# Modulations moved from a mixer's TensorE to three feed-forward stages' VectorE, memory keys moved into the inverse

## What is computed

```python
mod_lat = silu(c) @ w_mod + b_mod          # 1024 -> 6144, one row
mod_ctx = silu(c_ctx) @ w_mod + b_mod      # of this, only shift and scale before the mixer (2048) are used

def memory_cross_attention(h, m, w_q, w_kv, q_gain, k_gain, w_o):   # m = rms_norm(mem, xattn_mem_norm)
    q = rms_norm((h @ w_q).reshape(B, S, 4, 128), q_gain)
    kv = (m @ w_kv).reshape(B, M, 2, 4, 128)
    k, v = rms_norm(kv[:, :, 0], k_gain), kv[:, :, 1]
    s = einsum('bqhd,bkhd->bhqk', q, k) * 128 ** -0.5
    return einsum('bhqk,bkhd->bqhd', softmax(s), v).reshape(B, S, 512) @ w_o
```

## Time and profile before

| | |
|---|---|
| median of 3 runs | 2467.96 us (2465.76 to 2468.3) |
| span of the profiled execution | 2465.7 us, 41821 instructions |
| TensorE (PE) busy | 2246.6 us (91%) |
| weight loads (PEld), beside it | 2014.1 us (82%) |
| VectorE, ScalarE, GpSimd busy | 979.8, 1157.1, 1191.6 us |
| mean granted TensorE clock | 0.959 of full speed |
| DMA | 318.49 MB, 129 GB/s on the mean |

### The profile page before, as it was taken

The page is one execution under the profiler, slowest core; times in us unless marked ns, Lnnn a source line. Parts: engine busy times, 40 slices in busy tenths (PEclk is TensorE's granted clock), DMA queues, the critical chain, the costliest instruction groups (busy, mean ns, idle before and its releaser), DMA issues. The chain is left out here.

```text
span 2465.7 us, 41821 instructions
## 1 busy us (share of the span) xinstructions
PE 2246.6 (91%) x17916; PEld 2014.1 (82%) x17916; DVE 979.8 (40%) x1980; ACT 1157.1 (47%) x1651; POOL 1191.6 (48%) x304
## 2 busy tenths in 40 slices
PE   8998989899998999888989999897987777998998
PEld 7998865488998999785568999775866777998997
DVE  2321644324211220356242321256665777333540
ACT  5433632465433442543255543455883555553342
POOL 6774610074875877440053887332310000675784
PEclk9999999899999999999989999898998888999999
DMA  7554522253654555432333554331204111653552
GB/s 251 171 175 130 155 83 86 69 173 101 201 170 143 189 183 162 139 111 86 120 103 103 171 188 154 118 104 52 69 21 135 35 36 24 209 165 126 180 180 95
DMA packets 303958, 318.49 MB, mean 129 GB/s; under 512 B 7881, under 2 KB 295101, under 8 KB 303261
## 3 DMA queue, kind: packets, MB, share of 16 engines
q1 hardware_dynamic: 303773, 315.81, 39.8%
HBM read 312.58 MB, written 3.21 MB: 128 GB/s over the span
## 5 line engine op out<-in xcount | busy, mean ns | idle before, releaser
L370 POOL TENSOR_TENSOR slab_lo<-ring,slab_hi 128x2048 fp32r<-128x2048 f32 (+1 forms) x238 | 1073.5, 4527 | 762.7 <-ACT slab_hi L359 727.0
L359 ACT CAST slab_hi<-ring 128x2048 fp32r<-128x2048 f32 (+1 forms) x238 | 443.8, 1869 | 550.8 <-PE bank L440 278.8
L435 PE MATMUL bank<-ffn_h_hi,slab_hi 128*128 128x256 f32 x1344 | 331.2, 284 | 0.0
L436 PE MATMUL bank<-ffn_h_lo,slab_hi 128*128 128x256 f32 x1344 | 329.7, 283 | 0.0
L435 PEld LDWEIGHTS bank<-ffn_h_hi,slab_hi 128*128 128x128 f32 x1344 | 257.9, 192 | 0.5 <-issue 0.3
L436 PEld LDWEIGHTS bank<-ffn_h_lo,slab_hi 128*128 128x128 f32 x1344 | 258.0, 192 | 0.1
L402 PE MATMUL bank<-ffn_hidden_hi,slab_hi 128*128 128x256 f32 x704 | 199.3, 283 | 0.0
L403 PE MATMUL bank<-ffn_hidden_lo,slab_hi 128*128 128x256 f32 x704 | 199.2, 283 | 0.0
L404 PE MATMUL bank<-ffn_hidden_hi,slab_lo 128*128 128x256 f32 x704 | 199.2, 283 | 0.0
L440 PE MATMUL bank<-ffn_h_hi,slab_lo 128*128 128x256 f32 x1344 | 189.1, 283 | 4.4 <-POOL slab_lo L370 4.4
L440 PEld LDWEIGHTS bank<-ffn_h_hi,slab_lo 128*128 128x128 f32 x1344 | 173.3, 192 | 5.2 <-POOL slab_lo L370 5.2
(11 more groups left out here) (655 smaller groups left out, 5369.0 us busy)
## 6 DMA issues: line engine op xcount, KB each, us to landing
ring<-in_ffn_w_in SPq DMA_DIRECT2D x88, 1024.0 KB, 5.1
ring<-in_ffn_w_out SPq DMA_DIRECT2D x32, 1024.0 KB, 5.2
ring<-in_w_in SPq DMA_DIRECT2D x27, 1024.0 KB, 5.3
ring<-in_mix_w_in SPq DMA_DIRECT2D x24, 1024.0 KB, 5.4
ring<-in_w_mod SPq DMA_DIRECT2D x24, 1024.0 KB, 5.2
ring<-in_w_up SPq DMA_DIRECT2D x22, 1024.0 KB, 5.1
ring<-in_ffn_w_out SPq DMA_DIRECT2D x16, 768.0 KB, 4.4
ring<-in_mix_w_out SPq DMA_DIRECT2D x8, 1024.0 KB, 5.2
```

The lines of the kernel that those rows point to most:

```text
L359: act.copy(self.hi[i % self.PLACES][:, 0:w], K.ring[n % RING][:, 0:w]).then_inc(self.hi_ready, 1)
L370: pool.tensor_tensor(self.lo[i % self.PLACES][:, 0:w], place[:, 0:w], self.hi[i % self.PLACES][:, 0:w].bitcast(F32), ALU.subtract).then_in ...
L435: pe.matmul(out, w[0][:, k, col], act[0][:, k, :], start=(k == 0), stop=False)
L436: pe.matmul(out, w[0][:, k, col], act[1][:, k, :], start=False, stop=False)
```

## The change

1. The modulations leave the mixer. A new `Modulations` is given to three feed-forward stages (`mod_part` 0: ffn2 of layer 0, 1: ffn1 of layer 1, 2: ffn2 of layer 1). Each makes 2048 of the 6144 columns, in 16 pieces of 0.5 MB with two places of their own. VectorE adds weight tile times a scalar of `cs` into bank 7, and copies the sums out after a group is full; TensorE, after the stage's last output product, multiplies each 128 of these sums by a column of ones (`pe`), and VectorE copies the result. Part 0 makes both versions (latent and context) of the first 2048 columns, the other parts only the latent.
2. In the inverse's wait TensorE now projects the memory's keys: two slabs straight from the ring, as full float32 products (`feature_major`, L309), with the memory scaled by GpSimd (`MemoryKeys`). ScalarE copies them to `xkeys`.
3. The attention stage has no modulations in its steps, none ahead, no transposes behind, and loads no slabs.
4. The cross attention has 10 slabs: four of the output projection, values 0, queries 0 and 1, values 1 (half of it ahead of the steps, half in steps 0 and 1), two of the output. The sums of squares of keys come after the norm of x on ScalarE.

```diff
+class Modulations:
+    PIECES, PLACES = 16, 2
+    BANK = 7
+    def __init__(self, K, ctx, part):
+        self.K, self.part = K, part
+        self.both = part == 0
+        self.cols, self.groups = (HALF, 4) if self.both else (2 * HALF, 2)
+        self.a_group = KD // self.groups
+        self.count = self.PIECES // self.a_group
+        self.first = 0 if self.both else 2 * KD * part
+        self.place = [K.sb(f"mod_piece{i}", [P, self.groups, self.cols], ctx=ctx) for i in range(self.PLACES)]
+        self.sums = K.sb("mod_sums", [P, self.count, 2 * HALF], ctx=ctx)
...
+        again = part == 2
...
+    def eaten(self, p):
+        return self.base + p + 1 + p // self.a_group
+    def kept(self, g):
+        return self.base + (g + 1) * (self.a_group + 1)
+    def sync(self, sync, p):
+        K = self.K
+        g, h = divmod(p, self.a_group)
+        if p >= self.PLACES:
+            sync.wait_ge(self.steps, self.eaten(p - self.PLACES))
+        src = groups_of(K.a["w_mod_2"], h * self.groups, self.groups, self.first * P + g * self.cols, self.cols)
+        sync.dma_start(self.place[p % self.PLACES][:, :, :], src).then_inc(self.landed[p % self.PLACES], 16)
+    def dve(self, dve, p):
+        K, own, bank = self.K, self.K.dve_own, self.K.bank[self.BANK]
+        g, h = divmod(p, self.a_group)
+        dve.wait_ge(self.landed[p % self.PLACES], 16 * (self.landings + p // self.PLACES + 1))
+        for q in range(self.groups):
+            k, w = h * self.groups + q, self.place[p % self.PLACES][:, q, :]
+            for v in range(1 + self.both):
+                out = bank[:, v * self.cols:(v + 1) * self.cols]
+                if k == 0:
+                    last = dve.tensor_scalar(out, w, K.cs[:, k, v:v + 1], None, ALU.mult)
+                else:
+                    last = dve.scalar_tensor_tensor(out, w, K.cs[:, k, v:v + 1], out, ALU.mult, ALU.add)
+            if q < self.groups - 1:
+                own.after(dve, last)
+        last.then_inc(self.steps, 1)
+        dve.wait_ge(self.steps, self.eaten(p))
+        if h == self.a_group - 1:
+            dve.tensor_copy(self.sums[:, g, :], bank[:, :]).then_inc(self.steps, 1)
+            dve.wait_ge(self.steps, self.kept(g))
+    def pe(self, pe):
+        K, bank = self.K, self.K.bank[self.BANK]
+        pe.wait_ge(self.steps, self.kept(self.count - 1))
+        for t in range(4 * self.count):
+            g, j = divmod(t, 4)
+            last = pe.matmul(bank[:, t:t + 1], self.sums[:, g, j * P:(j + 1) * P], K.c("ones", n=1), start=True, stop=True)
+        last.then_inc(self.steps, 1)
+    def dve_end(self, dve):
+        K, n = self.K, 4 * self.count
+        dve.wait_ge(self.steps, self.kept(self.count - 1) + 1)
+        if self.both:
+            dve.tensor_copy(K.mod[:, 0:n // 2, :].rearrange("p (g j) v -> p g j v", j=2),
+                            K.bank[self.BANK][:, 0:n].rearrange("p (g v j) -> p g j v", v=2, j=2))
+        else:
+            dve.tensor_copy(K.mod[:, self.first:self.first + n, 0], K.bank[self.BANK][:, 0:n])
+def ffn_stage(K, tag, gain, opening=None, mod_part=None):
...
+                if mod is not None:
+                    for p in range(mod.PIECES):
+                        K.load_slabs(sync, n0 + 2 * p + RING + 1)
+                        mod.sync(sync, p)
...
                 ffn_out_pe(K, pe, split, hidden, x_updated, lambda: pe.wait_ge(product_ready, N))
+                if mod is not None:
+                    mod.pe(pe)
...
+                        if mod is not None:
+                            mod.dve(dve, i)
                 for jj in range(4):
+                    if mod is not None and jj < 3:
+                        for p in range(N + 2 * jj, min(N + 2 * jj + 2, mod.PIECES)):
+                            mod.dve(dve, p)
                     K.wait_slabs(dve, n0 + FK + 3 * (jj + 1))
                     for j in range(2):
                         k = 2 * jj + j
                         dve.scalar_tensor_tensor(K.x[:, k, :], K.bank[out_bank(jj, j)][:, 0:T], 0.5, K.x[:, k, :],
                                                  ALU.mult, ALU.add).then_inc(x_updated, 1)
+                if mod is not None:
+                    mod.dve_end(dve)
 def ffn_slabs(w_in, w_out):
...
-    slabs += [whole(K.a["w_mod_2"], l * (MOD_SLABS * HALF) + i * HALF) for i in range(MOD_SLABS)]
+    slabs += [whole(w("xattn_w_kv"), i * HALF) for i in range(2)]
     slabs += mix_xattn_slabs(K, l)
...
+class MemoryKeys:
+    SLABS = 2
+    def __init__(self, K, ctx, keys_ctx):
+        self.K, self.n0 = K, K.eaten
+        self.mem = K.sb("mem_scaled", [P, KD, T], ctx=ctx)
+        K.xkeys = K.sb("xkeys", [P, 2 * self.SLABS, T], ctx=keys_ctx, side="right")
+        self.scaled = K.pool_own.n + 1
+    def pool(self, pool):
+        K = self.K
+        for k in range(KD):
+            last = pool.tensor_scalar(self.mem[:, k, :], K.mem[:, k, :], K.col("xattn_mem_norm", KD)[:, k:k + 1], None, ALU.mult)
+        K.pool_own.on(last)
+    def pe(self, pe):
+        K = self.K
+        pe.wait_ge(K.pool_own.sem, self.scaled)
+        for n in range(self.SLABS):
+            K.slab_done(feature_major(K, pe, K.bank[n], view(K.next_slab(pe)), self.mem, KD, HALF))
+    def act(self, act):
+        K = self.K
+        for n in range(self.SLABS):
+            K.wait_slabs(act, self.n0 + n + 1)
+            act.copy(K.xkeys[:, pair_of(n), :], K.bank[n][:, :].rearrange("p (a t) -> p a t", a=2))
+def rwkv_stage(K, keys_ctx):
...
-        mod = Modulations(K, ctx)
...
+            keys = MemoryKeys(K, ictx, keys_ctx)
...
-                    K.load_slabs(sync, mod.n0 + mod.FIRST + RING)
+                    K.load_slabs(sync, keys.n0 + keys.SLABS + RING)
...
-                    mod.pe_first(pe)
+                    keys.pe(pe)
...
-                    inv.act(act, between=lambda i: mod.act_first(act) if i == 1 else None)
+                    inv.act(act, between=lambda i: keys.act(act) if i == 1 else None)
...
+                    keys.pool(pool)
...
-        attention_stage(K, lt, xt, unit, mod)
+        attention_stage(K, lt, xt, unit)
 class RwkvScan:
...
-class Modulations:
...
-            def _(sync):
-                K.load_slabs(sync, mod.n0 + MOD_SLABS + RING)
...
                 scan.pe(pe, 1)
-                for _ in range(mod.AHEAD):
-                    mod.some(pe)
                 for i in range(2):
                     pe.wait_ge(normed, 8)
...
                     scan.pe(pe, 2 + i)
...
-                att.pe(pe, between=lambda: mod.some(pe), mid_step=lambda i: scan.pe(pe, i + EARLY))
-                mod.pe_end(pe)
+                att.pe(pe, mid_step=lambda i: scan.pe(pe, i + EARLY))
...
-                att.act(act, at_step=lambda i: (mod.act(act, i, att.CALLS), scan.act(act, i + EARLY - 1)))
-                mod.act(act, KD * MOD_SLABS, 1)
+                att.act(act, at_step=lambda i: scan.act(act, i + EARLY - 1))
...
 def mix_xattn_slabs(K, l):
     w = lambda n: K.a[n][bass.ds(l, 1), :, :]
     slabs = [whole(w("mix_w_out"), i * HALF) for i in range(4)]
-    slabs += [whole(w("xattn_w_kv"), i * HALF) for i in range(2)]
+    slabs += [whole(w("xattn_w_kv"), 2 * HALF)]
     slabs += [whole(w("xattn_w_q"), i * HALF) for i in range(2)]
-    slabs += [whole(w("xattn_w_kv"), i * HALF) for i in range(2, 4)]
+    slabs += [whole(w("xattn_w_kv"), 3 * HALF)]
     slabs += [[(groups_of(w("xattn_w_out"), 0, 4, i * 512, 512), P, 0, 4, 512)] for i in range(2)]
     return slabs
...
     n0 = K.eaten
-    MIX, KEYS, QUERIES, VALUES = 0, 4, 6, 8
+    MIX, QUERIES, VALUES, OUT = 0, 5, (4, 7), 8
...
     with ExitStack() as ctx:
...
                 K.slab_done(feature_major_first(pe, split, K.bank[MIX], split.next_rounded(pe), y_parts))
-                for n in range(1, KEYS):
+                for n in range(1, 4):
                     K.slab_done(feature_major_late(pe, split, K.bank[MIX + n], split.next_rounded(pe), both(y_parts)))
                     pe.wait_ge(m_parts.lo_ready, 4)
                     sum_x(n - 1)
-                for i in range(2):
-                    K.slab_done(feature_major3(pe, K.bank[4 + i], split.next_view(pe), both(m_parts), KD, HALF))
-                    if i == 0:
+                w = split.next_view(pe)
+                for t in range(TT):
+                    last = token_major3(pe, K.bank[5][:, t * HALF:(t + 1) * HALF], w, both(m_parts), KD, HALF, tiles=(t,))
+                    if t == 0:
                         sum_x(3)
+                K.slab_done(last)
                 pe.wait_ge(x_parts.lo_ready, 4)
                 K.slab_done(feature_major3(pe, K.bank[6], split.next_view(pe), both(x_parts), KD, HALF))
                 sum_heads(0)
                 sum_heads(1)
-                pe.wait_ge(kv_copied, 1)
                 K.slab_done(feature_major3(pe, K.bank[4], split.next_view(pe), both(x_parts), KD, HALF))
                 sum_heads(2)
-                pe.wait_ge(kv_copied, 2)
```

(71 more changed lines are left out.)

83 lines of the change are left out of this document (12 added, 71 removed).

## The result

| | before | after |
|---|---|---|
| median, 12 runs each | 2468.28 us (2465.74 to 2484.05) | 2480.05 us (2472.9 to 2484.17) |
| ratio to the kernel before | | 1.0034, 95% interval 1.0018 to 1.005 |
| span of the profiled execution | 2465.7 us | 2480.3 us |
| mean granted TensorE clock | 0.959 | 0.920 |

What follows compares the result with a forecast made beforehand. TensorE was taken as the bound. Attention stage -53.1, keys -1.6, cross attention -16.8 and feed-forward tails +13.3 sum to -58.2 us; from the 2465.7 us span, plus 2.3 to the median, this gave 2410 us, range 2398 to 2440.

Steps and rivals of the forecast that it cites:

- What bounds the kernel: Whole kernel: TensorE, busy for 2246.6 of 2465.7 us, is the path; in the attention steps its queue is full.
- The removed work: Attention steps 0 to 9: without 28 modulation batches, 26.6 us, they take 39.0 us; gains 29.0 and 25.6 us.
- rival (a): Attention steps: hand-over between engines shows 0.8 us of waiting per step in place of batches, +16, 2426 us; chance 0.12.
- The clock's share: Attention stage: TensorE's clock falls after the opened wait, some 10 us low, 4 us per layer; +6.7 us in all.
- Full queue at 1.00 in layer 1 from 1165 on: Layer 1's attention steps before the change, at full clock: cited against the clock staying low through one layer's steps.
- Rival (c): Attention stages of both layers: clock stays low from 378 to the end, +68, 2478 us, 0.4% slower; chance 0.04.
- Rival (e): Keys' projection: TensorE's work not hidden but on the path in full, 14 us per layer, 2434; chance 0.05 with (d).
- Keys: Wait for the inverse: the memory's key products replace modulation work and nearly fit; -1.6 us, bounds -3.2 to +4.4.
- Cross attention: Cross attention stage: queries end one slab earlier and half of values 1 fills a wait; -8.4 per layer, -16.8 us.
- Feed-forward: Three feed-forward stages: VectorE's modulation pieces fit its 4.47 us idle times; cost 0, at most 2 us per stage.
- rival (d): Feed-forward stages: slabs land late behind the modulation pieces, +42, 2452 us; chance 0.05 together with (e).
- The tails' term: Behind three feed-forward stages: narrow products with ones on the path, 6.9 + 3.2 + 3.2 = +13.3 us, bounds +12 to +16.

Runs made afterwards that it cites:

- Filling of equal length, wide or narrow: Changed kernel with idle products in 28 former batch places per layer: one of 512 columns each, 2482.45 us; or four of one column each, 2571.04 us.
- the run without the narrow tails: Changed kernel with one narrow product instead of 32, 16 and 16 behind the three feed-forward stages: 2456.67 us, ratio 0.9946.
- the narrow filling: Changed kernel with four idle products of 128x128 by one column in each of 28 former batch places: 2571.04 us, ratio 1.0387.
- the early filling: Changed kernel with eight wide idle products in the wait and 18 more per layer, mostly around the first steps: 2446.44 us, ratio 0.9907.

## Why the prediction was wrong

**What bounds the kernel** was right. TensorE was the path in the steps, and stayed it in every version.

**The removed work** was sized rightly. At the full level, the steps with 16 idle products took 53.8 us. At 0.86 each that leaves 40.0 us of the steps' own work, against 38.0 from the batches' removal and 39.0 in the sum. In the changed kernel no new wait took their place: the busy column is full in all ten steps, so rival (a) isn't what happened. Whether waits would show at the full level without idle products was never seen, since every run that held that level had them in the steps.

**The clock's share** is the step that failed. It said: a fall is likely, "I take some 10 us of it after the gap, 4 us per layer". The steps cost 68.47 and 67.80 us in place of 39, so 58 us more in both layers, of the 63 that the attention stage missed; that is also beyond the prediction's own sign of being wrong, steps above 50 us. The size of the low level against the full one was about right (1.77 forecast; 68.47 over 40.0 is 1.71). Its length was not. Two rows bear on the length, and I weighed both wrongly. "Full queue at 1.00 in layer 1 from 1165 on" was taken as what a full queue does. It was what a queue with batches does: 112 of its records there are L1988, 256 columns each. Taking them out changed the very thing on which that row rested. And 392 to 400 at 0.51 with TensorE full, which the text names as speaking against the rule, was the warning: full was not enough.

The text named a statement of the Trainium skill (TensorE: Matmul & The Clock Gate, "What's actually happening"), that the low state is the default and activity releases it, and read the busy column as the activity. Filling of equal length, wide or narrow, gave 75.2 and 116.0 us in layer 0: the traces agree in that the level fell in a wait (low from 377.0), and disagree with my reading that busy time in the profile is what leads out of it.

**Rival (c)**, "it stays low in both layers' stages", is what happened, at 2478 against 2480.05. It had 0.04. Its price, +60 in the steps and +16 before them less the 8 already in the sum, was worked out. Its chance was wrong: nothing in the rows showed that the steps without the batches could hold the level. That its time came so near is partly luck: in the traces the attention stage came out 5 us below its price, while the tails, the keys and the untouched parts came out 10 above their places in the sum. Rival (e) has a slip that changes nothing: 14 us per layer on top of 2410 is 2438, not 2434.

**Keys**: right in mechanism. Layer 1 fitted as said. Layer 0 took 15.77 us, nearly the upper bound of 16.1, and the inverse's first products, without an idle time ahead of them, gave back what it cost: 0.0 and -0.2 in place of the sum's -1.6.

**Cross attention**: -17.4 against -16.8, by the steps as told; first scores at 552.46, 7.3 us nearer to the start of the stage than before, with TensorE waiting for 5.39 us (3.81 before).

**Feed-forward**: VectorE's pieces cost nothing, as said. From the first product of layer 0's second stage to the end of its last output product it is 192.5 us in both traces, with the pieces of up to 3.6 us in VectorE's idle time. The window over the stretch of the earlier trace rows, moved by the 4 us by which the stage starts earlier:

```profile
636.00:682.00 46.00, 46.00 (x385) 46.00 (x385) 25.71 (x50) 19.11 (x17) 36.88 (x9) 1.00 0.71 233
```

DMA share 0.71 and 233 GB/s, where about 0.7 and 230 were worked out; rival (d) is out. The tails' term was too small, +16.4 in the traces for +13.3. The second gave +5.5 where 3.2 stood, although its products took what was forecast: the sum of squares behind it ran at the low level, 5.41 us for 3.72. Taking them out gave back 21.7 us by the medians. The same term was missing as in the steps, what narrow products do to the level of those behind them.

Layer 1's projections took 3.0 us more in the changed kernel's profile, and the level is what the traces show there. The projections of layer 1 in the changed kernel, where the level was low twice for a short time (from 1080.2 and from 1090.4), then in the kernel before:

```profile
1022.89:1114.03 91.14, 86.05 (x642) 80.26 (x641) 43.02 (x46) 49.65 (x71) 51.03 (x11) 0.96 0.48 150
```

```profile
1012.58:1100.73 88.15, 83.05 (x642) 77.27 (x641) 42.13 (x46) 49.50 (x71) 51.07 (x11) 1.00 0.50 156
```

With one such stretch, in the run without the narrow tails, they took 1.5 us more. What drops the level there stays open, and so does how much of the differences of some us between medians is the level elsewhere in the run. The kernel before alone spread over 2465.7 to 2487.7 us on one chip.

## What to carry to other kernels

Before work is taken off a full TensorE queue, ask what is left in it: here the work that was removed was the wide part, and what was left ran at 1.2 GHz with a busy share of 100%. A row at the full level is evidence only for the mix of work in that row, so read the granted clock beside the busy column, and look for a stretch without the work that is to go. Where it can't be real work, an idle wide product can pay: 18 of 0.86 us in each layer, and eight more in a wait, turned 1.0034 into 0.9907, on different chips, each against the kernel before.

## What the runs showed of the hardware

- TensorE ran at 0.50 for 88.7 us on end in the changed kernel (from 377.0, in the wait ahead of the steps) and for 136.5 us with the narrow filling (from 376.9), with not one idle microsecond in the ten steps that lie within.
- Products of one column with full weights: placed ahead of the last output slabs they started at 764.12, 0.99 us behind output products at the full level, and the level was low from 765.7, with no idle time in them. 64 records took 12.32 us there, 32 took 3.63 us where the level held.
- One product of 512 columns in each of the steps 3 to 9 held the level in one execution and lost it in another (from 425.6 for 23.9 us); with two, both layers ran their ten steps in 59.83 us. The mean granted clock was 0.957 with the early filling, and 0.920 in the changed kernel.
